# Input projections: bias tiles copied after the weight requests, two q/k weight tiles split ahead, first v weights split within the q/k block

## The chip, the cores and the metric

The kernel runs on one NeuronCore of a Trainium2 chip. The metric is the device time of one execution in microseconds (us); the three timed runs of the kernel before gave 1987.66, 1990.0 and 1991.83 us, median 1990.0 us. Engines are called PE (TensorE), PEld (its weight loads), ACT (ScalarE), DVE (VectorE), POOL (GpSimd) and SP (SyncE).

## What is computed

One decoder layer over 512 prompt tokens and 32 sample tokens, model width 1024. Only its first part matters here:

```python
u = rmsnorm(h, g_attn)
z = u @ w_in              # q, k, v of 8 forgetting heads | q, k, v of 8 dilated heads | 8 forget logits
logf = log_sigmoid(fz + b_f)          # 8 per token; summed along the tokens for the attention bias
o_fox = attention(qa, ka, va, cumulated logf)
o_dil = dilated attention(qb, kb, vb, rel_bias table)
h = h + [rms(o_fox) | rms(o_dil)] @ w_out
h = h + PEER(rmsnorm(h))              # 16384 single-neuron experts, top 16 per head
```

k, v and logf of all tokens are outputs as well. The bias table `rel_bias` gives, per dilated head, a 128 x 512 tile of biases and its turned twin; attention reads them from DRAM.

## The kernel before

The work is a row of blocks. Each block gives every engine its own instruction list, and the engines meet at the end of the block; inside it only semaphores order them. Every fp32 product is made of three matmuls (`mm3`, lines 225 to 227) of operands split in two: ACT copies the weights to a rounded high part (`hi`), DVE subtracts it from the weights for the low part (`lo`). So each weight tile goes DMA, ACT, DVE, PE.

The norm block (lines 298 to 386) turns the normalised tokens into `xhi`, `xlo`. It also loads the first two q/k weight tiles and writes the bias rows to DRAM (lines 334, 335).

The q/k block (lines 391 to 529) makes q and k transposed, in 8 turns m = 0..7. Each turn has two tiles of 128 columns, u = 0 (q) and u = 1 (k), of 512 KB each. PE's list is `product(0, 0)`, then a loop whose pass is `product(m, 1)`, `product(m+1, 0)`, `turn_k(m)`, and after the seven passes `product(7, 1)`, `turn_k(7)`. A product is 48 matmuls of 272 columns. `turn_k` transposes k back to token rows in 5 transposes, which DVE copies to `kn` (lines 472, 473) and POOL writes to the k outputs. POOL waits for each output to land before it frees `kn`, and for the last one before the block ends (line 529).

SP's list in this block begins with two transfers from DRAM to DRAM of 2 MB each, which spread the bias rows to the tiles `tile_dram` (line 414). Behind them come the loads of the 14 other q/k tiles, each waiting for the low split of the tile whose buffer it takes (lines 417, 418), and the loads of the first two v weight tiles of 1 MB each (line 420).

ACT's turn (lines 434 to 445) is: split hi of (m, 1), evacuate product (m, 0) to `qkT`, split hi of (m+1, 0), evacuate product (m, 1) to `kz`. DVE's turn (lines 464 to 473) is: split lo of (m, 1), split lo of (m+1, 0), wait for `kz` and copy it to `qkT`, wait for `turn_k(m)` and copy `kn`.

The v block (lines 531 to 612) makes v in 4 chunks of 256 columns. For each chunk PE does 5 token tiles of 24 matmuls into five accumulators `pv_acc` (line 277), and DVE copies each to `v` (line 533). `token_rows_product` (line 229) holds the lists of that product. PE waits for the low split of the chunk (`lo_done`, line 272) and for its accumulator to be free (`out_done`, line 275); the semaphore `out_done` is first raised to 5 by DVE in `first_on_vector` (line 257). DVE's list in the block is: `first_on_vector` (that raise, two low splits of v), the chain of the forget gate that turns the logits into `logf` and `cum` (lines 581 to 596, with ACT at lines 558 to 565), `on_vector` (the evacuations, and the low splits of chunks 2 and 3). ACT's list is two high splits of v (line 249), its gate steps, and the other high splits. SP's transfers of line 547, 548 and 241 wait for the end of the gate chain.

After it comes a barrier of all engines (line 616) and the attention block, where SP waits for the two bias transfers (line 724) and reads tiles from the fifth head pair on.

Of the kernel before, what the change touches and what calls it, by code (L numbers as in the profile page):

```python
# [32 lines left out]
P = 128  # L33
# [6 lines left out]
TT = SEQ // P + 1  # L40
# [28 lines left out]
def build(nc, A, O):  # L69
# [21 lines left out]
    with ctx:  # L91
# [134 lines left out]
            nc.tensor.matmul(out, a_hi, b_lo, start=False, stop=False)  # L226
            return nc.tensor.matmul(out, a_lo, b_hi, start=False, stop=last)  # L227

        def token_rows_product(st, tag, xhi, xlo, w, wld, w_dram, w_tiles, evacuate):


            CW = 256
            whi = sb(st, tag + "_whi", [P, 2, KD, CW], F32R)
            wlo = sb(st, tag + "_wlo", [P, 2, KD, CW], F32R)
            acc = [ps(st, f"{tag}_acc{t}", [P, CW]) for t in range(TT)]
            hi_done, lo_done, mm_done, out_done = (brief(f"{tag}_{n}") for n in ("hi_done", "lo_done", "mm_done", "out_done"))

            def on_sync(sp):
                for chunk in range(2, w_tiles):
                    sp.wait_ge(lo_done, chunk - 1)  # L240
                    sp.dma_start(w[:, chunk % 2], w_dram[chunk]).then_inc(wld[chunk % 2], 16)


            def on_scalar(act, chunks=range(w_tiles)):
                for chunk in chunks:
                    act.wait_ge(wld[chunk % 2], 16 * (chunk // 2 + 1))
                    if chunk >= 2:
                        act.wait_ge(mm_done, (chunk - 1) * TT)
                    nc.scalar.activation(whi[:, chunk % 2], w[:, chunk % 2], ACT.Copy).then_inc(hi_done, 1)

            def split_lo(dve, chunk):
                dve.wait_ge(hi_done, chunk + 1)
                nc.vector.tensor_tensor(wlo[:, chunk % 2], w[:, chunk % 2], whi[:, chunk % 2].bitcast(F32),
                                        ALU.subtract).then_inc(lo_done, 1)

            def first_on_vector(dve):
                dve.sem_inc(out_done, TT)
                split_lo(dve, 0)
                split_lo(dve, 1)

            def on_vector(dve):
                for chunk in range(w_tiles):
                    for t in range(TT):
                        if t == 2 and 1 <= chunk < w_tiles - 1:
                            split_lo(dve, chunk + 1)
                        dve.wait_ge(mm_done, chunk * TT + t + 1)
                        evacuate(t, chunk, acc[t]).then_inc(out_done, 1)

            def on_tensor(pe):
                with pe.Fori(0, w_tiles // 2) as j:  # L270
                    for u in range(2):
                        pe.wait_ge(lo_done, 2 * j + u + 1)
                        for t in range(TT):

                            pe.wait_ge(out_done, (2 * j + u) * TT + t + 1)
                            for k in range(KD):
                                last = mm3(acc[t][:], xhi[:, k, t * P:(t + 1) * P], xlo[:, k, t * P:(t + 1) * P],
                                           whi[:, u, k], wlo[:, u, k], k == 0, k == KD - 1)
                            last.then_inc(mm_done, 1)

            return on_sync, on_scalar, first_on_vector, on_vector, on_tensor


# [104 lines left out]
        w_early = sb(proj, "pv_w", [P, 2, KD, 256])  # L388
        w_loaded = [brief(f"pv_wld{u}") for u in range(2)]
        zf = ps(proj, "zf", [NH, 2, SEQ])  # L390
        with ExitStack() as st:
            w = w_qk
            whi = sb(st, "pwhi", [P, 2, KD, P], F32R)
# [14 lines left out]
            @block.sync  # L408
            def _(sp):

                sp.wait_ge(rows_done, 32)
                for turned, rows_of in enumerate((bass.AP(bias_dram.tensor, NH * DIST + P - 1, [[DIST, NH], [-1, P], [1, SEQ]]),
                                                  bass.AP(turned_dram.tensor, P - 1, [[DIST, NH], [-1, P], [1, SEQ]]))):
                    sp.dma_start(tile_dram[turned], rows_of).then_inc(tiles_done, 16)
                with sp.Fori(0, NH - 1) as m:
                    for u in range(2):
                        sp.wait_ge(lo_done, 2 * m + u + 3)
                        sp.dma_start(w[:, u], A["w_qk"][2 * m + 2 + u]).then_inc(wld[u], 16)
                for u in range(2):
                    sp.dma_start(w_early[:, u], A["w_v"][u]).then_inc(w_loaded[u], 16)  # L420


            @block.scalar
            def _(act):
                act.sem_inc(ev_done, 2)
                act.wait_ge(f_ld, 32)
                nc.scalar.activation(wfhi[:], wf[:], ACT.Copy).then_inc(f_hi, 1)

                def split(m, u):
                    act.wait_ge(wld[u], 16 * m + 16)  # L430
                    act.wait_ge(mm_done, 2 * m + u + 1)
                    nc.scalar.activation(whi[:, u], w[:, u], ACT.Copy).then_inc(hi_done, 1)

                def turn(m, last):
                    split(m, 1)
                    act.wait_ge(mm_done, 2 * m + 3)
                    nc.scalar.activation(qkT[:, 2 * m, :].rearrange("p (a b) -> p a b", a=2),
                                         zp[0][:, :, :HALF], ACT.Copy).then_inc(ev_done, 1)
                    if not last:
                        split(m + 1, 0)  # L440
                    act.wait_ge(mm_done, 2 * m + 4)
                    act.wait_ge(kt_done, m + 1)
                    act.wait_ge(kcopied, m + 1)
                    nc.scalar.activation(kz[:].rearrange("p (a b) -> p a b", a=2),
                                         zp[1][:, :, :HALF], ACT.Copy).then_inc(ev_done, 1)

                split(0, 0)
                with act.Fori(0, NH - 1) as m:
                    turn(m, False)
                turn(NH - 1, True)  # L450

            @block.vector
            def _(dve):
# [8 lines left out]
                    nc.vector.tensor_tensor(wlo[:, u], w[:, u], whi[:, u].bitcast(F32), ALU.subtract).then_inc(lo_done, 1)  # L462

                def turn(m, last):
                    split(m, 1)
                    if not last:
                        split(m + 1, 0)
                    dve.wait_ge(ev_done, 2 * m + 4)
                    nc.vector.tensor_copy(qkT[:, 2 * m + 1, :], kz[:]).then_inc(kcopied, 1)
                    dve.wait_ge(kt_done, m + 2)  # L470
                    dve.wait_ge(kn_free, m + 1)
                    nc.vector.tensor_copy(kn[:, 0:TT - 1], kp[:, 0:TT - 1])
                    nc.vector.tensor_copy(kn[:NS, TT - 1], kp[:NS, TT - 1]).then_inc(kn_done, 1)

                split(0, 0)
                with dve.Fori(0, NH - 1) as m:
                    turn(m, False)
                turn(NH - 1, True)
# [50 lines left out]
                pool.wait_ge(k_out, 32 * NH)  # L529

        with ExitStack() as st:
            def keep_v(t, chunk, acc):
                return nc.vector.tensor_copy(v[:, t, bass.ds(chunk * 256, 256)], acc[:])

            on_sync, on_scalar, first_on_vector, on_vector, on_tensor = token_rows_product(st, "pv", xhi, xlo, w_early, w_loaded, A["w_v"], 4, keep_v)
            gz, ga, ge, gu, gl, gd, gw = (sb(st, "g" + n, [NH, NT]) for n in ("z", "a", "e", "u", "l", "d", "w"))
            logf = sb(st, "logf", [NH, NT])
            cum = sb(st, "cum", [NH, SEQ])
# [5 lines left out]
            @block.sync  # L544
            def _(sp):
                sp.wait_ge(f_dve, 10)
                sp.dma_start(logf_dram, logf[:]).then_inc(f_out, 16)
                sp.dma_start(cum_dram, cum[:]).then_inc(f_out, 16)
                on_sync(sp)
                sp.wait_ge(f_dve, 11)  # L550
                sp.dma_start(O["lfp"].rearrange("(t p) h -> p t h", p=P), lf[:, 0:TT - 1]).then_inc(f_out, 16)
                sp.dma_start(O["lfs"], lf[:NS, TT - 1]).then_inc(f_out, 16)
                sp.wait_ge(f_out, 64)

            @block.scalar
            def _(act):
                on_scalar(act, range(2))
                nc.scalar.activation(gz[:].rearrange("p (a b) -> p a b", a=2), zf[:, :, :HALF], ACT.Identity,
                                     bias=bf[:]).then_inc(f_act, 1)
                act.wait_ge(f_act, 1)  # L560
# [2 lines left out]
                nc.scalar.activation(ge[:], ga[:], ACT.Exp, scale=-1.0).then_inc(f_act, 1)  # L563
                act.wait_ge(f_dve, 1)
                nc.scalar.activation(gl[:], gu[:], ACT.Ln).then_inc(f_act, 1)
                on_scalar(act, range(2, 4))

            @block.vector
            def _(dve):
                first_on_vector(dve)  # L570
                count = [0]

                def step(ins):
# [20 lines left out]
                nc.vector.tensor_tensor_scan(cum[:], ga[:, :SEQ], logf[:, :SEQ], 0.0, ALU.mult, ALU.add).then_inc(f_tr, 1)  # L594
                dve.wait_ge(f_tr, 2)
                step(nc.vector.tensor_scalar(cum[:], cum[:], -SCALE8, None, ALU.mult))
                on_vector(dve)
                dve.wait_ge(f_mm, 1)
                nc.vector.tensor_scalar(cumT[:], lp[:, TT:], 1.0 / SCALE8, None, ALU.mult)
                nc.vector.tensor_copy(lf[:, 0:TT - 1], lp[:, 0:TT - 1])  # L600
# [1 line left out]

            @block.tensor
            def _(pe):
                on_tensor(pe)
                pe.wait_ge(f_dve, 10)
                for t in range(TT - 1):
                    nc.tensor.transpose(lp[:, TT + t], cum[:, t * P:(t + 1) * P], ident[:NH, :NH])
# [1536 lines left out]
```

## Time and profile before

| | |
|---|---|
| median of 3 runs | 1990.0 us (1987.66 to 1991.83) |
| the profiled execution | 1990.47 us, span 1988.8 us from first to last instruction |
| PE busy | 1738.9 us, 87% of the span, 9914 matmuls |
| PEld busy | 1519.9 us, 76% |
| DVE, ACT, POOL busy | 1442.5, 689.4, 594.2 us |
| mean granted PE clock | 0.941 of full |

Start times are microseconds from the start of the span. The norm block ends at about 33 us, the q/k block's last PE instruction at 177.73, the v block's at 247.53. A timeline row gives the start, the duration, the engine, line and operation, what it writes and reads, and in brackets how long its engine had been idle before it and who released it. An engine that waits little is not yet the one that sets the end: one has to ask for each idle stretch of PE what came last.

### The profile page before, as it was taken

How to read it: one execution, taken by the hardware profiler on the slowest of the kernel's cores; microseconds unless marked ns; L12 is line 12 of the kernel's file. 1: busy time of each engine (PE TensorE's matmuls, PEld its weight loads, DVE VectorE, ACT ScalarE, POOL GpSimd, SP SyncE). 2: the span in 40 equal slices, each digit the busy share in tenths (PEclk: the TensorE clock that was granted, in tenths of full speed). 3: DMA queues.
4: the chain of work that ended last, by engine and by line, in shares of the span. 5: the costliest groups of instructions: out<-in, count | busy, mean ns of one | idle time of the engine just before them, and what ended most of it. 6: DMA issues, size and time to landing. Idle time of an engine off the chain costs nothing. (4 is left out here: it accounts for less than half of the span.)

```text
span 1988.8 us, 30525 instructions
## 1 busy us (share of the span) xinstructions
PE 1738.9 (87%) x9914; PEld 1519.9 (76%) x9914; DVE 1442.5 (73%) x3310; ACT 689.4 (35%) x912; POOL 594.2 (30%) x520
## 2 busy tenths in 40 slices
PE   5786988788799999996989989989499999999995
PEld 4786943347688888886988888888488888888883
DVE  3123346624467666677999999999698999999985
ACT  3112022202333333322545445445233333333333
POOL 0000072000134443434333333333333333333330
PEclk9888989889799999998999999999799999999997
DMA  4321182053133333333998998998899999999993
GB/s 142 111 80 70 43 265 75 16 213 122 63 109 109 122 108 108 112 108 127 331 362 327 349 362 327 338 366 326 305 384 383 385 385 385 384 385 385 385 385 115
DMA packets 195174, 470.30 MB, mean 236 GB/s; under 512 B 17922, under 2 KB 100482, under 8 KB 192558
## 3 DMA queue, kind: packets, MB, share of 16 engines
q1 hardware_dynamic: 124014, 240.30, 34.1%
q0 software_dynamic: 50944, 178.96, 24.4%
q10 hardware_dynamic: 20160, 50.34, 6.4%
q8 instruction: 30, 0.49, 0.1%
q14 instruction: 26, 0.21, 0.0%
HBM read 411.97 MB, written 61.32 MB: 238 GB/s over the span
## 5 line engine op out<-in xcount | busy, mean ns | idle before, releaser
L225 PE MATMUL hp<-mid_hi,uhi 128*128 128x384 f32 x1024 | 365.3, 357 | 40.6 <-POOL ulo L1284 31.1
L226 PE MATMUL hp<-mid_lo,uhi 128*128 128x384 f32 x1024 | 354.5, 346 | 0.0
L227 PE MATMUL hp<-mid_hi,ulo 128*128 128x384 f32 x1024 | 352.4, 344 | 0.0
L225 PE MATMUL va<-vhi,ahi 128*128 128x512 f32 x768 | 300.0, 391 | 21.3 <-DVE alo L1923 21.3
L226 PE MATMUL va<-vlo,ahi 128*128 128x512 f32 x768 | 299.5, 390 | 0.0
L227 PE MATMUL va<-vhi,alo 128*128 128x512 f32 x768 | 299.5, 390 | 0.0
L1939 POOL DMA_INDIRECT gathered<-in_v_experts,idx_row x160 | 186.3, 1164 | 329.6 <-DVEq L1894 289.2
L1644 POOL DMA_INDIRECT gathered<-in_u_rows,idx_row x160 | 169.9, 1062 | 300.8 <-DVE hrow L1699 199.8
L225 PEld LDWEIGHTS hp<-mid_hi,uhi 128*128 128x128 f32 x1024 | 201.3, 197 | 46.7 <-POOL ulo L1284 33.3
L1280 ACT ACTIVATE uhi<-uw 128x1024 fp32r<-128x1024 f32 x128 | 135.5, 1059 | 236.3 <-PE hp L227 143.6
L226 PEld LDWEIGHTS hp<-mid_lo,uhi 128*128 128x128 f32 x1024 | 200.7, 196 | 0.0
L227 PEld LDWEIGHTS hp<-mid_hi,ulo 128*128 128x128 f32 x1024 | 200.4, 196 | 0.0
L1868 ACT ACTIVATE vhi<-vw 128x1024 fp32r<-128x1024 f32 x128 | 134.8, 1053 | 151.9 <-DMA vw<-in_v_experts 147.8
L225 PEld LDWEIGHTS va<-vhi,ahi 128*128 128x128 f32 x768 | 144.7, 188 | 52.1 <-issue 22.0
L1699 DVE CUSTOM_DVE_ANT_0 gathered<-gathered,x2p 128x1024 f32<-128x1024 f32 x150 | 177.6, 1214 | 9.2 <-DMA gathered<-in_u_rows,idx_row 5.5
L1284 POOL TENSOR_TENSOR ulo<-uw,uhi 128x1024 fp32r<-128x1024 f32 x54 | 131.4, 2440 | 171.1 <-ACT uhi L1280 171.1
L1918 DVE TENSOR_TENSOR vlo<-vw,vhi 128x1024 fp32r<-128x1024 f32 x128 | 156.2, 1220 | 17.1 <-ACT vhi L1868 16.9
L226 PEld LDWEIGHTS va<-vlo,ahi 128*128 128x128 f32 x768 | 144.7, 188 | 30.1
L227 PEld LDWEIGHTS va<-vhi,alo 128*128 128x128 f32 x768 | 144.6, 188 | 30.1
L1891 DVE SCALAR_TENSOR_TENSOR acc<-gathered,crow,acc 128x1024 f32<-128x1024 f32 x128 | 164.2, 1282 | 0.0
L1622 PE MATMUL ggp<-og,oh 128*128 128x128 f32 x768 | 107.8, 284 | 36.9 <-DVE og L1690 36.9
L1622 PEld LDWEIGHTS ggp<-og,oh 128*128 128x128 f32 x768 | 98.2, 194 | 50.3 <-DVE og L1690 50.3
(318 smaller groups left out, 3279.9 us busy)
## 6 DMA issues: line engine op xcount, KB each, us to landing
uw<-in_u_experts SPq DMA_DIRECT2D x128, 512.0 KB
vw<-in_v_experts SPq DMA_DIRECT2D x128, 512.0 KB
hidden_values<-gelu_out ACTq DMA_DIRECT2D x128, 192.0 KB
gate_matrix<-gst ACTq DMA_DIRECT2D x12, 2048.0 KB
hd<-hidden_values SPq DMA_DIRECT2D x32, 768.0 KB
gt<-gate_matrix SPq DMA_DIRECT2D x32, 768.0 KB
pw<-in_w_qk SPq DMA_DIRECT2D x16, 512.0 KB, 3.8
qw<-in_w_query SPq DMA_DIRECT2D x16, 512.0 KB, 4.3
```

The costliest lines, as they stand in the source:

```text
L225: nc.tensor.matmul(out, a_hi, b_hi, start=first, stop=False)
L226: nc.tensor.matmul(out, a_hi, b_lo, start=False, stop=False)
L227: return nc.tensor.matmul(out, a_lo, b_hi, start=False, stop=last)
L1280: nc.scalar.activation(uhi[:, i], uw[:, i], ACT.Copy).then_inc(u_hi, 1)
L1284: nc.gpsimd.tensor_tensor(ulo[:, i], uw[:, i], uhi[:, i].bitcast(F32), ALU.subtract).then_inc(u_lo, 1)
L1622: last = nc.tensor.matmul(gp[i % 2][:, k], oh[:, i % RING, k], og[:, i % RING, k], start=True, stop=True)
L1644: nc.gpsimd.indirect_dma_start(gb[:, b], None, u_table, bass.IndirectOffsetOnAxis(ap=idx_row[:, slot, b:b + 1], axis=0)).then_inc(gathered ...
L1699: nc.vector.tensor_tensor_reduce(out=gb[:, b], in0=gb[:, b], in1=x2p[:, b // SG], scale=1.0, scalar=0.0, op0=ALU.mult, op1=ALU.add, accum_ ...
L1868: nc.scalar.activation(vhi[:, c], vw[:, c], ACT.Copy).then_inc(s["vhi"], 1)
L1891: nc.vector.scalar_tensor_tensor(acc0[:], gb[:, c], crow[:, q, c:c + 1], acc0[:], ALU.mult, ALU.add).then_inc(s["s0"], 1)
L1918: nc.vector.tensor_tensor(vlo[:, c], vw[:, c], vhi[:, c].bitcast(F32), ALU.subtract).then_inc(s["vlo"], 1)
L1939: nc.gpsimd.indirect_dma_start(gb[:, b], None, v_table, bass.IndirectOffsetOnAxis(ap=idx_row[:, slot, b:b + 1], axis=0)).then_inc(gathered ...
```

## The change

Three moves, all in the input projections; no arithmetic is added or left out.

1. On SP the two transfers of the bias tiles go from the front of its q/k list to its end, behind the loads of the 14 q/k tiles and the two v tiles.
2. On DVE, tile (0, 1) is split ahead of the loop, and each turn splits (m+1, 0) before the copy of `kz` and (m+1, 1) right after it, instead of (m+1, 1) at the start of the next turn, behind the `kn` copies.
3. The high and low splits of v chunks 0 and 1 go from the front of the v block into the last turn of the q/k block: ACT's behind the evacuation of product (7, 0), DVE's in the place of the split it no longer has there. For that the `pv` split buffers are allocated earlier. The first raise of `out_done` goes from `first_on_vector` to the front of `on_vector`.

```diff
@@ token_rows_product
             def first_on_vector(dve):
-                dve.sem_inc(out_done, TT)
                 split_lo(dve, 0)
                 split_lo(dve, 1)
 
             def on_vector(dve):
+                dve.sem_inc(out_done, TT)
                 for chunk in range(w_tiles):
@@ q/k block, sync
-                sp.wait_ge(rows_done, 32)
-                for turned, rows_of in enumerate((bass.AP(bias_dram.tensor, NH * DIST + P - 1, [[DIST, NH], [-1, P], [1, SEQ]]),
-                                                  bass.AP(turned_dram.tensor, P - 1, [[DIST, NH], [-1, P], [1, SEQ]]))):
-                    sp.dma_start(tile_dram[turned], rows_of).then_inc(tiles_done, 16)
                 with sp.Fori(0, NH - 1) as m:
                     for u in range(2):
                         sp.wait_ge(lo_done, 2 * m + u + 3)
                         sp.dma_start(w[:, u], A["w_qk"][2 * m + 2 + u]).then_inc(wld[u], 16)
                 for u in range(2):
                     sp.dma_start(w_early[:, u], A["w_v"][u]).then_inc(w_loaded[u], 16)
-
+                sp.wait_ge(rows_done, 32)
+                for turned, rows_of in enumerate((bass.AP(bias_dram.tensor, NH * DIST + P - 1, [[DIST, NH], [-1, P], [1, SEQ]]),
+                                                  bass.AP(turned_dram.tensor, P - 1, [[DIST, NH], [-1, P], [1, SEQ]]))):
+                    sp.dma_start(tile_dram[turned], rows_of).then_inc(tiles_done, 16)
@@ q/k block, scalar, turn
-                    if not last:
+                    if last:
+                        v_split_hi(act, range(2))
+                    else:
                         split(m + 1, 0)
@@ q/k block, vector, turn
-                    split(m, 1)
-                    if not last:
+                    if last:
+                        v_split_first(dve)
+                    else:
                         split(m + 1, 0)
                     dve.wait_ge(ev_done, 2 * m + 4)
                     nc.vector.tensor_copy(qkT[:, 2 * m + 1, :], kz[:]).then_inc(kcopied, 1)
+                    if not last:
+                        split(m + 1, 1)
...
                 split(0, 0)
+                split(0, 1)
@@ v block, scalar
-                on_scalar(act, range(2))
                 nc.scalar.activation(gz[:].rearrange("p (a b) -> p a b", a=2), zf[:, :, :HALF], ACT.Identity,
                                      bias=bf[:]).then_inc(f_act, 1)
@@ v block, vector
-                first_on_vector(dve)
...
                 step(nc.vector.tensor_scalar(cum[:], cum[:], -SCALE8, None, ALU.mult))
-                on_vector(dve)
+                v_evacuate(dve)
```

`v_split_hi`, `v_split_first`, `v_evacuate` are the new names of `on_scalar`, `first_on_vector`, `on_vector`.

## Rows read from the trace of the kernel before

**Rows 1.** Busy time by engine in the q/k and v stretches (windows view).

```profile
core 0: us, PE busy (x) PEld busy (x) DVE busy (x) ACT busy (x) POOL busy (x), PEclk, DMA share, GB/s
33.06:177.73 144.67, 120.67 (x856) 115.55 (x856) 27.93 (x38) 24.87 (x32) 9.39 (x14) 0.91 0.30 108
177.73:247.53 69.80, 58.84 (x489) 58.62 (x489) 28.51 (x38) 12.68 (x10) 1.31 (x2) 0.90 0.09 35
```

**Rows 2.** What PE waited for, 33 to 250: total us, times, longest.

```profile
PE zp L225 <- DVE pwlo L462: 23.3, 8, 8.1
PE pv_acc L225 <- DVE pv_wlo L253: 11.0, 1, 11.0
```

**Rows 3.** Timeline of PE, its restarts and its transposes.

```profile
60.62 0.59 PE L225 MATMUL zp<-xhi,pwhi 128*128 128x272 f32 x1 [8.10 <-DVE pwlo L462]
69.46 0.71 PE L501 MATMUL kp<-ident,kz 128*128 128x128 f32 x5
72.35 0.39 PE L225 MATMUL zp<-xhi,pwhi 128*128 128x272 f32 x1 [2.18 <-DVE pwlo L462]
168.44 0.39 PE L225 MATMUL zp<-xhi,pwhi 128*128 128x272 f32 x1 [2.10 <-DVE pwlo L462]
...
188.69 0.58 PE L225 MATMUL pv_acc<-pv_whi,xhi 128*128 128x256 f32 x1 [10.96 <-DVE pv_wlo L253]
```

**Rows 4.** PE alone, windows from restart to end of products: busy, clock, DMA.

```profile
60.62:69.46 8.84, 8.84 (x48) 0.66 0.18 61
72.35:86.00 13.65, 13.65 (x96) 0.87 0.30 97
88.89:101.01 12.12, 12.12 (x97) 1.00 0.31 110
168.44:176.25 7.81, 7.80 (x48) 0.78 0.13 36
188.69:192.69 4.00, 4.00 (x18) 0.50 0.02 4
```

**Rows 5.** Timeline of ACT.

```profile
58.17 1.06 ACT L432 ACTIVATE pwhi<-pw 128x1024 fp32r<-128x1024 f32 x1 [10.90 <-DMA pw<-in_w_qk]
80.71 1.06 ACT L432 ACTIVATE pwhi<-pw 128x1024 fp32r<-128x1024 f32 x1
184.31 3.71 ACT L249 ACTIVATE pv_whi<-pv_w 128x2048 fp32r<-128x2048 f32 x2 [7.40 <-PEq L391]
187.93 0.69 ACT L558 ACTIVATE gz<-zf,bf 8x544 f32<-8x544 f32 x1
```

**Rows 6.** Timeline of DVE.

```profile
80.97 0.44 DVE L469 COPY qkT<-kz 128x544 f32 x1 [7.62 <-ACT kz L444]
86.75 0.69 DVE L472 COPY kn<-kp 128x512 f32<-128x512 f32 x1 [5.33 <-PE kp L501]
87.55 2.34 DVE L462 TENSOR_TENSOR pwlo<-pw,pwhi 128x1024 fp32r<-128x1024 f32 x2
186.25 4.49 DVE L253 TENSOR_TENSOR pv_wlo<-pv_w,pv_whi 128x2048 fp32r<-128x2048 f32 x2 [7.61 <-ACT pv_whi L249]
201.94 0.42 DVE L596 TENSOR_SCALAR cum<-cum 8x512 f32<-8x512 f32 x1
218.95 0.42 DVE L533 COPY v<-pv_acc 128x256 f32<-128x256 f32 x1 [2.38 <-PE pv_acc L227]
221.75 0.42 DVE L533 COPY v<-pv_acc 128x256 f32<-128x256 f32 x1 [2.38 <-PE pv_acc L227]
```

**Rows 7.** SP's queue: the bias transfers and what stands behind them.

```profile
33.24 0.78 SPq L414 DMA_DIRECT2D bias_tiles<-bias_rows  x1
38.30 115.58 SPq L418 DMA_DIRECT2D pw<-in_w_qk  x14
```

**Rows 8.** All engines, 36 to 48, with only the bias transfers moving.

```profile
36.00:48.00 12.00, 12.00 (x98) 10.78 (x97) 0.10 (x1) 0.63 (x1) 0.00 (x0) 1.00 0.53 197
```

**Rows 9.** Transfers issued 151 to 166, median us from issue to landing.

```profile
pv_w<-in_w_v SPq DMA_DIRECT2D x2, 1024.0 KB, 7.2
pw<-in_w_qk SPq DMA_DIRECT2D x1, 512.0 KB, 3.8
out_kwp<-kn POOLq DMA_DIRECT2D x1, 256.0 KB, 3.5
```

More of the change, by code:

```diff
@@ L227, in mm3, with token_rows_product @@
             return nc.tensor.matmul(out, a_lo, b_hi, start=False, stop=last)
-        def token_rows_product(st, tag, xhi, xlo, w, wld, w_dram, w_tiles, evacuate):
+        def token_rows_product(st, tag, xhi, xlo, w, wld, w_dram, w_tiles, evacuate, acc):
             CW = 256
@@ L234, in token_rows_product @@
             wlo = sb(st, tag + "_wlo", [P, 2, KD, CW], F32R)
-            acc = [ps(st, f"{tag}_acc{t}", [P, CW]) for t in range(TT)]
             hi_done, lo_done, mm_done, out_done = (brief(f"{tag}_{n}") for n in ("hi_done", "lo_done", "mm_done", "out_done"))
@@ L390, in build, with keep_v @@
         zf = ps(proj, "zf", [NH, 2, SEQ])
+        v_acc = []
+        def keep_v(t, chunk, acc):
+            return nc.vector.tensor_copy(v[:, t, bass.ds(chunk * 256, 256)], acc[:])
+        v_loads, v_split_hi, v_split_first, v_evacuate, v_products = token_rows_product(
+            proj, "pv", xhi, xlo, w_early, w_loaded, A["w_v"], 4, keep_v, v_acc)
         with ExitStack() as st:
@@ L531, in build @@
         with ExitStack() as st:
-            def keep_v(t, chunk, acc):
-                return nc.vector.tensor_copy(v[:, t, bass.ds(chunk * 256, 256)], acc[:])
-            on_sync, on_scalar, first_on_vector, on_vector, on_tensor = token_rows_product(st, "pv", xhi, xlo, w_early, w_loaded, A["w_v"], 4, keep_v)
+            v_acc += [ps(st, f"pv_acc{t}", [P, 256]) for t in range(TT)]
             gz, ga, ge, gu, gl, gd, gw = (sb(st, "g" + n, [NH, NT]) for n in ("z", "a", "e", "u", "l", "d", "w"))
@@ L548, in _ @@
                 sp.dma_start(cum_dram, cum[:]).then_inc(f_out, 16)
-                on_sync(sp)
+                v_loads(sp)
                 sp.wait_ge(f_dve, 11)
@@ L565, in _ @@
                 nc.scalar.activation(gl[:], gu[:], ACT.Ln).then_inc(f_act, 1)
-                on_scalar(act, range(2, 4))
+                v_split_hi(act, range(2, 4))
             @block.vector
             def _(dve):
-                first_on_vector(dve)
                 count = [0]
@@ L604, in _ @@
             def _(pe):
-                on_tensor(pe)
+                v_products(pe)
                 pe.wait_ge(f_dve, 10)
```

## The prediction

> **What bounds the kernel now.** I read the windows view first. It cuts the span where PE's work changes: the q/k stretch takes 144.67 us with PE busy for 120.67, the v stretch 69.80 us with 58.84 busy [rows 1]. No other engine is busy for half of either, and the DMA engines move little, so PE sets both stretches and the question is what it waits for and at which clock it runs. The table of waits answers the first: 23.3 us of idle PE in 8 waits for DVE's low split of a q/k tile, the longest 8.1, and one wait of 11.0 for the low split of v [rows 2]. The timeline places them: 8.10 us before 60.62, once; 2.18 us in each of the six loop passes whose product follows a `turn_k`, and 2.10 before the last product, at 168.44 [rows 3]. The clock answers the second. The reader should lay the passes of two products beside each other: 12.12 us where the granted clock is 1.00, 13.65 us where it is 0.87 [rows 4]; of the six, four (from 72.35, 103.90, 120.44 and 136.98) last 13.65 and two 12.12. Clock 1.00 is 2.4 GHz, and the 0.50 of the first 4 us of the v products is 1.2 GHz [rows 4]; every stretch at the low level follows an idle stretch of PE. So a stall is paid twice here, in idle time and in slow matmuls behind it.
>
> **The opening stall (SP's move).** The third q/k tile reached SP's queue at 38.30, behind two transfers of 2 MB that were issued from 33.24 on [rows 7]. ACT waited 10.90 us for it and could split it only at 58.17 [rows 5]. After the change SP waits only for the low split of tile (0, 0) and asks for the third tile near 35; a tile takes about 3.8 us to land [rows 9], so it is there before product (0, 0) frees its buffers. The stall of 8.10 goes, and product (1, 0) takes half of 12.12, 6.06 us, instead of the 8.84 from 60.62 to 69.46 at mean clock 0.66 [rows 3, 4]. Worth 8.10 + 2.78 = 10.88 us. What is late next there: nothing; both splits of that tile take 2.3 us and a product of 6 us runs meanwhile.
>
> **The stall in each turn (DVE's move).** DVE does `kn`, then two splits in 2.34 us, and only the second is the one that PE waits for [rows 6]. It could have been done long before: ACT's high split of (m+1, 1) runs at 80.71, right after `kz` [rows 5], while DVE copies at 80.97 and then sits idle for 5.33 us until `turn_k` [rows 6]. After the change the split runs from about 81.8 to 83.0 in that picture, 3 us before the product then running ends, with `turn_k`'s 0.71 more as slack; the split of (m+2, 0) comes behind the `kn` copies, about 3 us after the product that frees it, under a product of 6.06. So I cost both splits at nothing. All seven stalls go, 6 x 2.18 + 2.10 = 15.2. With PE never idle I take the clock to stay at 1.00 as it does from 88.89, so four passes give 1.53 each, 6.1, and the last product 7.81 - 6.06 = 1.75 [rows 4]. Together 23.0 us.
>
> Two costs that the stall may have covered have no row of their own. One is the loop's way back. In the v block PE also loops, and DVE's evacuations at the last tile of chunk 1 and the first of chunk 2, on the two sides of that way back, start 2.80 us apart [rows 6], as within a chunk; its bounds are 0 and the 2.18 it could hide in, and I take 0, the nearest row. The Trainium skill (Advanced Engine Details and Errata, section Control Flow Timing) puts a compare-and-branch at about 108 ns; an estimate from it is 0.8 us over seven passes, which the sum leaves out, since the row shows nothing of it. The other is the load of the next tile: from the split that frees its buffer to the product that frees the split buffers it has about 10 us, against 3.8.
>
> PE's end in the q/k block thus goes from 177.73 to 177.73 - 10.9 - 23.0 = 143.8.
>
> **The end of the q/k block.** The v splits now stand in the last turn. On ACT, 3.71 us behind the evacuation of product (7, 0) [rows 5] end near 4.4 us into the 6.8 before product (7, 1) is done. On DVE, `kn` of turn 6 ends 1.7 us after product (7, 0), the two splits of v take 4.49 [rows 6] from about 2.8, and end near 7.2, when `kz` is just written at about 7.5. They cost nothing, with 0.3 us to spare on DVE. If that cover were gone they would delay the last `kn` by their excess. The v weights are requested with the last q/k tile, near 120, and need 7.2 us [rows 9]; they are wanted at 136.
>
> Behind them SP now issues the bias transfers, at about 121. They alone keep 0.53 of the DMA engines busy at 197 GB/s [rows 8], so 4.19 MB take 21 us; after the weights have landed near 128.5 this gives an end near 150. The transposes of turns 6 and 7 end near 136 and 144, and their outputs leave some 2 us later, within that time, and the block cannot end before the last has landed. Before, the block switched at 184.31, 6.58 us after PE's last instruction [rows 1, 5]. What the mixture costs, no row shows. The nearest has an output of 256 KB landing in 3.5 us with weight loads issued around it [rows 9], nearly no cost; the other end is an output that waits until the copies are through, which for the last one is 3 us and for that of turn 6, which holds up the next `kn` copy, up to 6. I take 1, near the row, and keep 0 to 6. The first row that speaks for more is that half of the engines is busy all the time [rows 8]. The Trainium skill (DMA: Bandwidth & Descriptors, section Queues, rings and completion order) says that an engine alternates between its queues packet by packet, so an output would be interleaved and not stand behind the whole copy; by that rule the sum would stay in the lower half of my bounds. SP itself waits for nothing after its last issue, and attention asks for the tiles only much later.
>
> The v block therefore begins at 143.8 + 6.6 + 1 = 151.4 instead of 184.31.
>
> **The v block: a wait that takes the place of the one removed.** Before, PE waited for ACT and DVE to split chunk 0: 188.69 - 184.31 = 4.38 us after the block began [rows 3, 5]. That is gone. But PE also needs `out_done`, and its first raise now stands behind the gate chain in DVE's list. Everything in the block waits for it: PE's four chunks, all evacuations, and with them the end. The chain's length is in the trace: ACT's first gate step starts at 187.93 and DVE's last ends at 201.94 + 0.42 = 202.36 [rows 5, 6], 14.43 us, a pure chain of ACT and DVE steps with no DMA and no PE in it. Before, it ran beside PE's chunk 0. Now ACT starts it with the block, and PE starts at 14.5 us instead of 4.4: 10.1 us lost. From there PE has its 58.84 us of work as before [rows 1], which already hold the slow start (4.00 us at 0.50 after 10.96 idle [rows 3, 4]); PE's idle stretch is about 22 us now, and the restart after 8.10 idle lost 2.78 us, that is 5.6 at the low level, some 2 more than here, so this term is good to 1 us. Loads and splits of chunk 2 start with the chain's end as before and have all of chunk 0 to hide in.
>
> **The sum.** 33.9 gained in the q/k block, 10.1 lost in the v block, 1 for the shared DMA engines: 22.8 us. The attention block begins behind a barrier of all engines and PE's end at 247.53 comes near 224.7, so all later work, none of which was requested earlier, moves by the same amount. The profiled execution took 1990.47 us for a span of 1988.8; it should come to about 1967.7, and the median of 1990.0 to 1967.2, forecast 1967.
>
> **The rivals.**
> (a) The stalls shrink but stay. If a way back, a semaphore or the split still holds PE for about half of the 2.18 in each turn, 7.7 us stay, and so does the slow clock behind them, 7.9: gain 7.2, 1983. For it: small idle stretches did lower the clock in four of six passes. Against: the slack of 3 us above. 10%.
> (b) The seven turns gain nothing, because each wait is taken over by another (a tile load, `kn` behind POOL's outputs). Then only the opening's 10.9 stands against 10.1 + 1: 1990. Against: a tile lands in 3.8 us and an output in 3.5 [rows 9], in a turn of 12.8. 3%.
> (c) The k outputs are held up by the bias copies to the far end, 4 to 6 us: 1970 to 1972. 8%.
> (d) PE is not held by the gate chain, since the accumulators are free in fact and something else raises the count. Then 14 us more are gained: 1953. The lists say otherwise. 3%.
> (e) Slower: after the long idle stretch at the front of the v block the clock does not come back. At the 1.2 GHz level 18 matmuls took 4.00 us [rows 4], so a chunk's 120 take 26.7, against 14.0 at full clock (five evacuations 2.80 apart [rows 6]). Four chunks cost 51 us more, of which 2 are in the sum already: 1967 + 49 = 2016. It decides from two chunks at the low level on, 25 us. Against it: after 8.10 and after 10.96 us of idle the clock was back within 6 us. 4%.
> The forecast itself has 72%.
>
> **The numbers.** Low end: no DMA cost (1966), 2 for a shorter slow start, 2 for the spread of runs: 1962. High end: 6 of DMA cost (1972), and 5 for the loop, the branch and spread: 1977. The range holds the forecast and (c) and a part of (a). About 0.2%, 4 us, is what a measurement of this kernel can tell from no change. Faster by more than that: 0.72 + 0.10 + 0.08 + 0.03 = 0.93; within: 0.03 (b); slower: 0.04 (e).
>
> **What would show it.** In the profile after: PE's waits for `pwlo` gone from the q/k stretch (now 23.3); every pass of two products 12.1 us at clock 1.00; the last transposes near 144; a switch of blocks near 151; then a PE wait of about 21 to 22 us ended by DVE's `cum` or by no named instruction, with the first v product right behind the gate chain; PE's end of v near 225. If passes last 13 us or more, the clock step failed; if the block switches at 155 or later, the DMA step; if v starts within 5 us of the switch, the reading of `out_done` was wrong.

## The result and the profile after

The changed kernel took 1971.31 us (median of 4 runs, 1968.57 to 1978.38) against 1988.83 for the kernel before on the same occasion: ratio 0.9913, interval 0.989 to 0.9936, 17.5 us less. The forecast was 1967, range 1962 to 1977. The profiled execution took 1978.38 us, the slowest of the four, with a span of 1976.8. Six further runs of the same kernel (e1, below) had a median of 1969.73. Line numbers differ from the kernel before: 414 is 425, 472 is 481, 501 is 511, 558 is 564, 596 is 601, and the evacuation of v at 533 is 392; behind line 600 they are 5 higher.

The windows view of the q/k and v stretches of the kernel after, the rows that answer to [rows 1]:

```profile
core 0: us, PE busy (x) PEld busy (x) DVE busy (x) ACT busy (x) POOL busy (x), PEclk, DMA share, GB/s
32.28:141.36 109.08, 108.37 (x856) 105.21 (x856) 33.70 (x40) 28.48 (x34) 9.37 (x14) 1.00 0.38 131
141.36:225.93 84.57, 59.45 (x490) 59.22 (x489) 24.31 (x36) 9.07 (x8) 1.31 (x2) 0.84 0.12 45
```

The q/k stretch went from 144.67 us to 109.08 and PE is busy in all but 0.7 of it, at a mean granted clock of 1.00. The v stretch grew from 69.80 to 84.57 with the same work in it. PE's timeline shows where:

```profile
166.48 0.58 PE L225 MATMUL pv_acc<-pv_whi,xhi 128*128 128x256 f32 x1 [25.12 <-DVEq L259]
232.42 0.80 PE L766 MATMUL S<-qkT 64*128 64x128 f32 x4 [6.49 <-ACT identr L889]
```

Between `turn_k(7)` and the first v product PE waits 25.12 us, before 10.96 [rows 3], and the one that releases it is DVE's queue at line 259, which is the raise of `out_done`. The timelines of SP, DVE, POOL and ACT show what the 25.12 us are made of:

```profile
118.33 0.81 SPq L421 DMA_DIRECT2D pv_w<-in_w_v  x2
119.19 0.79 SPq L425 DMA_DIRECT2D bias_tiles<-bias_rows  x1
120.02 9.12 SPq L425 DMA_DIRECT2D bias_tiles<-turned_bias_rows  x1
...
141.95 0.69 DVE L481 COPY kn<-kp 128x512 f32<-128x512 f32 x1 [0.92 <-POOLq L538]
144.29 0.52 POOL L536 DMA_DIRECT2D out_kws<-kn  x1
151.94 0.70 ACT L564 ACTIVATE gz<-zf,bf 8x544 f32<-8x544 f32 x1 [11.39 <-PEq L396]
165.96 0.41 DVE L601 TENSOR_SCALAR cum<-cum 8x512 f32<-8x512 f32 x1
```

The block switches at 151.94, 10.58 us behind PE's last q/k instruction (6.58 before), and the gate chain runs from there to 166.37, 14.43 us as before [rows 5, 6]; PE starts 0.1 us later.

A loop pass of the q/k block, and the first 4 us of the v products (PE alone, against [rows 4]):

```profile
58.06:70.63 12.57, 12.57 (x103) 1.00 0.33 106
120.90:133.40 12.50, 12.50 (x103) 1.00 0.73 284
166.48:170.48 4.00, 4.00 (x18) 0.50 0.57 199
```

These passes hold the transposes too: from one evacuation of q to the next 12.57 us, where before it was 15.0 or 16.5. The transposes take 0.46 us of it, the time from their start to that of the next product:

```profile
57.77 0.71 PE L511 MATMUL kp<-ident,kz 128*128 128x128 f32 x5
58.23 0.37 PE L225 MATMUL zp<-xhi,pwhi 128*128 128x272 f32 x1
```

PE's end in the v block came from 247.53 to 225.93, 21.6 us sooner. Only 12.0 of them are left in the span of this execution. Where they went is the second question of the experiments. Most was lost at once, in the first 24 us of attention; the kernel before and then the kernel after, PE alone from its first attention matmul on:

```profile
253.98:277.98 24.00, 23.47 (x117) 0.85 0.94 317
```

```profile
232.42:256.42 24.00, 23.92 (x76) 0.55 0.94 315
```

A mean clock of 0.85 means 7.2 us at 1.2 GHz, one of 0.55 means 21.6. PE got through 117 matmuls before and through 76 after in the same time. The first reciprocal of attention (line 849, then 854) starts 25.5 us behind the block's constants before, 31.3 us after: 5.8 us gone. The other 3.8 us went in small amounts behind it: 1.5 in the rest of attention, 2.3 in the blocks after it.

### The profile page after: what moved, and what is told of

The parts are those of the page before. It is cut to its first block and busy times, and to the rows that moved or that the text cites. A ratio compares the mean times of both kernels' runs of the same rounds, so it can differ in the third digit from the quotient of the medians.

```text
span 1976.8 us, 30524 instructions
## 1 busy us (share of the span) xinstructions
PE 1736.0 (88%) x9914; PEld 1514.8 (77%) x9914; DVE 1444.3 (73%) x3310; ACT 688.9 (35%) x912; POOL 594.3 (30%) x520
## 5 line engine op out<-in xcount | busy, mean ns | idle before, releaser
L225 PEld LDWEIGHTS hp<-mid_hi,uhi 128*128 128x128 f32 x1024 | 201.1, 196 | 47.1 <-POOL ulo L1289 33.9
## 6 DMA issues: line engine op xcount, KB each, us to landing
hd<-hidden_values SPq DMA_DIRECT2D x32, 768.0 KB, 12.7
gt<-gate_matrix SPq DMA_DIRECT2D x32, 768.0 KB, 16.4
```

The source lines that it names most:

```text
L225: nc.tensor.matmul(out, a_hi, b_hi, start=first, stop=False)
```

## The experiments

All runs are compared with the kernel before run beside them; the 95% interval of a ratio reaches 0.15 to 0.27% to either side, which is 3 to 5 us.

**e1: the changed kernel again.** No edit.

> The changed kernel once more, nothing altered. In its first profile PE's end in the v block came 21.6 us sooner than before, but the span was only 12.0 us shorter: 5.8 us were lost in the first 30 us of attention, where the granted clock stood at 0.50 for 22 us instead of 7.6. Theory A (the clock's return after an idle stretch varies from run to run): this profile loses another amount there, between 0 and 6 us, the span moves with it, and the median is near 1969. Theory B (the change causes that loss): the low clock at the start of attention lasts about 22 us again and the span is near 1977.

Measured: 1969.73 us (6 runs, 1966.04 to 1973.94), ratio 0.9898 (0.9878 to 0.9917), span of the profile 1972.4. PE's end of v at 225.44. PE alone over the first 24 us of attention:

```profile
231.92:255.92 24.00, 24.00 (x84) 0.61 0.94 313
```

About 18.5 us at the low level (by quarters of a microsecond) and not 21.6, the first reciprocal 4.2 us late and not 5.8. Neither theory is settled by it: the length changes for one and the same kernel, but it is long again. PE's wait before v was 24.45 us here.

**e8: the kernel before again**, for the same question.

> The kernel before once more, for a second profile of the start of attention. Theory A (how long the clock stays at 0.50 after the switch to attention changes from run to run, whatever the kernel): a length other than the 7.2 us of its first profile, between 6 and 22. Theory B (the long stretches of 13 to 22 us belong to the kernels whose v splits were moved): about 7 us again.

Measured: 1990.32 us (8 runs, 1985.1 to 1992.41), ratio 1.000 (0.9986 to 1.0015).

```profile
253.91:277.91 24.00, 23.71 (x95) 0.72 0.95 312
```

About 13.5 us at the low level where the first profile of the same kernel had 7.2, and 95 matmuls instead of 117. The first reciprocal of attention came 2.2 us later for it, the end of the span 1.5. So the length changes from execution to execution for the kernel before too; theory B's "about 7 again" is wrong. Over all profiles of this study the mean clock of those 24 us was 0.85, 0.72, 0.86 (e3) and 0.85 (e4) where the v splits stay in the v block and PE waits 11 to 13 us at its front, and 0.55, 0.61, 0.73 (e2), 0.84 (e5), 0.86 (e6), 0.60 (e7), 0.72 (e9) and 0.72 (e10) for the kernels with the moved splits. Both groups spread. That the moved splits make the long stretches more frequent is neither shown nor excluded by so few.

**e2: `out_done` raised ahead of the gate chain**, in the changed kernel:

```diff
@@ token_rows_product
+            def raise_free(dve):
+                dve.sem_inc(out_done, TT)
+
             def on_vector(dve):
-                dve.sem_inc(out_done, TT)
@@ v block, vector
+                v_raise(dve)          # ahead of the gate chain
                 count = [0]
```

> The changed kernel with the first raise of out_done at the very front of DVE's list in the v block, ahead of the gate chain, and nothing else altered. Theory: PE's 25 us wait before the v products is the last kn output and the switch (10.6 us) plus the gate chain (14.5 us); with the raise ahead of it PE starts within 0.5 us of the switch, the chain hides beside chunk 0 (16 us), and PE's end of v comes 14.2 us sooner: median near 1957. Rival: the v products cannot start sooner for another reason (instruction lists, PSUM still read by the gate, the split weights): no gain, 1971. Second rival: DVE frees no accumulator until the chain ends, so chunk 1 is held up: more than 1 us of PE idle behind chunk 0, gain under 12.

Measured: 1954.24 us (5 runs, 1952.96 to 1958.44), ratio 0.9832 (0.9812 to 0.9852). Waits of PE and the first evacuation on DVE:

```profile
PE pv_acc L225 <- DVEq L259: 10.4, 1, 10.4
```

```profile
152.27 0.70 ACT L566 ACTIVATE gz<-zf,bf 8x544 f32<-8x544 f32 x1 [11.22 <-PEq L398]
166.75 0.42 DVE L394 COPY v<-pv_acc 128x256 f32<-128x256 f32 x1
```

PE's wait fell from 25.12 to 10.43 us: v starts with the switch, 0.04 us behind ACT's first gate step. The gate chain still takes its 14.4 us, but it ends at 166.72 while PE is in chunk 0, and PE has no second wait, so the accumulators come free in time. PE's end of v is at 211.02, 14.9 us sooner than in the changed kernel; the median is 15.5 us under that of e1, which ran beside it. The order of two entries in DVE's list is worth almost as much as the whole change gained.

**e3: SP's move alone**, on the kernel before.

```diff
-                sp.wait_ge(rows_done, 32)
-                for turned, rows_of in enumerate((...)):
-                    sp.dma_start(tile_dram[turned], rows_of).then_inc(tiles_done, 16)
                 with sp.Fori(0, NH - 1) as m:
...
+                sp.wait_ge(rows_done, 32)
+                for turned, rows_of in enumerate((...)):
+                    sp.dma_start(tile_dram[turned], rows_of).then_inc(tiles_done, 16)
```

> The kernel before with SP's move alone (bias transfers behind the weight loads). Theory: the stall of 8.1 us before product (1, 0) and its slow clock go (10.9 us), the six stalls of 2.18 stay, and the last k outputs are not held up, since the turns are longer and the bias transfers end before them, or by at most 4 us: 1978 to 1982. Rival: the loop's first pass inherits the stall (the third tile is still late): no gain, 1989.

Measured: 1981.93 us (11 runs, 1979.26 to 1985.8), ratio 0.996 (0.9946 to 0.9975), 7.7 us less. Waits of PE:

```profile
PE zp L225 <- DVE pwlo L462: 15.2, 7, 2.2
PE pv_acc L225 <- DVE pv_wlo L253: 12.8, 1, 12.8
```

The wait of 8.1 is gone, the seven of 2.2 stay, and the wait before v is 12.8 instead of 11.0. PE's last q/k instruction ends at 166.58, 11.15 us sooner; the forecast's term was 10.9. PE's end of v is only 9.75 us sooner, at 237.78, since the bias copies now touch the end of the block: its last small output landed 4.0 us after its issue, against 2.2 before, and the block switches 8.45 us behind PE's last q/k instruction instead of 6.58.

**e4: DVE's order alone**, on the kernel before.

```diff
                 def turn(m, last):
-                    split(m, 1)
                     if not last:
                         split(m + 1, 0)
                     dve.wait_ge(ev_done, 2 * m + 4)
                     nc.vector.tensor_copy(qkT[:, 2 * m + 1, :], kz[:]).then_inc(kcopied, 1)
+                    if not last:
+                        split(m + 1, 1)
...
                 split(0, 0)
+                split(0, 1)
```

> The kernel before with DVE's order alone (tile (m+1, 1) split behind the kz copy). Theory: all seven stalls of 2.1 to 2.2 us and the low clock behind them go, while the opening stall stays: passes of 12.6 us at clock 1.00, 23 us less, 1966. Rival (small stalls cost only themselves, the clock drops anyway): 15 us less, 1974.

Measured: 1965.41 us (5 runs, 1961.82 to 1968.39), ratio 0.9876 (0.9856 to 0.9897), 24.3 us less, more than the whole change. Waits of PE, and PE alone from 78.00, well behind the opening stall, to the end of the products (the clock is back at 1.00 by 68):

```profile
PE pv_acc L225 <- DVE pv_wlo L253: 11.0, 1, 11.0
PE zp L225 <- DVE pwlo L462: 8.1, 1, 8.1
```

```profile
78.00:152.45 74.45, 74.45 (x599) 1.00 0.34 114
```

The seven small waits are gone and 74 us run without a gap at full clock. This answers the rival, by which small stalls cost only themselves: the seven waits sum to 15.2 us, but the gain to PE's end of v is 22.95 (224.58 against 247.53), or 23.9 from the start of the q/k work, which came 0.9 us later in this execution. The q/k stretch itself shrank by 24.7: 15.2 of waits, 7.9 of the clock that no longer falls [rows 4] and 1.6 of shorter transposes; 0.8 of it was lost again in the v block.

**e5: the v part alone**, on the kernel before. The changed kernel, with these two lists as they were before:

```diff
@@ q/k block, sync: the bias transfers in front again
@@ q/k block, vector, turn
+                    split(m, 1)
                     if last:
                         v_split_first(dve)
...
-                    if not last:
-                        split(m + 1, 1)
...
                 split(0, 0)
-                split(0, 1)
```

> The kernel before with the third part of the change alone (v splits in the last q/k turn, out_done raised behind the gate chain); SP's and DVE's order as before. Theory: the q/k block ends as before, the v products start 14.5 us behind the switch instead of 4.4, so 10.1 us slower: 2000. Rival (the chain would have held up PE before as well, by the evacuations): within 2 us of 1990.

Measured: 1997.68 us (6 runs, 1995.11 to 2001.95), ratio 1.0047 (1.0029 to 1.0065), 8.9 us slower.

```profile
PE pv_acc L225 <- DVEq L259: 21.5, 1, 21.5
```

Taken alone this part is a loss: PE's wait before v is 21.46 us instead of 10.96. The 10.5 us are the forecast's 10.1 and 0.3 more: the switch is 6.9 us behind PE's last q/k instruction and not 6.58, although no copy runs there.

**e6: the bias transfers in the v block**, from the changed kernel, to separate the 4 us at the switch.

```diff
@@ q/k block, sync: the wait on rows_done and the two transfers removed
@@ v block, sync
+                sp.wait_ge(rows_done, 32)
+                for turned, rows_of in enumerate((...)):
+                    sp.dma_start(tile_dram[turned], rows_of).then_inc(tiles_done, 16)
                 sp.wait_ge(f_dve, 10)
                 sp.dma_start(logf_dram, logf[:]).then_inc(f_out, 16)
```

> The changed kernel with the two bias transfers at the front of SP's list in the v block. Theory: the 10.6 us between PE's last q/k instruction and the switch hold 4 us of k outputs that share the DMA engines with the bias copies; with the copies behind the switch it is 6.6 again, as before the change, and nothing in the v block needs the DMA engines soon: 4 us less than the changed kernel, 1966. Rival: the 4 us are the time that SP or the v splits take, not the sharing: switch still 10 us behind PE, 1970. If the loads of v chunk 2 are held up by the copies, PE waits behind chunk 1.

Measured: 1967.8 us (6 runs, 1965.58 to 1971.99), ratio 0.9894 (0.9877 to 0.9912); the change itself had 1971.3 and 1969.7, so in the medians the difference is no more than hinted at. The profile shows the earlier switch. ACT's first step behind the switch, and PE's wait:

```profile
148.87 0.70 ACT L564 ACTIVATE gz<-zf,bf 8x544 f32<-8x544 f32 x1 [7.74 <-PEq L396]
```

```profile
PE pv_acc L225 <- DVEq L259: 21.5, 1, 21.5
```

The switch is 6.91 us behind PE's last q/k instruction (141.96), not 10.58. The transfers themselves say why; issued in the last turn, median us from issue to landing, kernel after and then e6:

```profile
out_kwp<-kn POOLq DMA_DIRECT2D x1, 256.0 KB, 2.9
out_kws<-kn POOLq DMA_DIRECT2D x1, 16.0 KB, 5.3
```

```profile
out_kwp<-kn POOLq DMA_DIRECT2D x1, 256.0 KB, 2.8
out_kws<-kn POOLq DMA_DIRECT2D x1, 16.0 KB, 2.2
```

The large output is hardly disturbed by the copies; the small one, 16 KB behind it, lands 3.1 us later, and it is the last thing the block waits for. The kernel before, whose last outputs meet no copy, and turn 6 of the kernel after (issued at 136.25, 12 us before the copies end near 148.6) show the same two figures:

```profile
out_kws<-kn POOLq DMA_DIRECT2D x1, 16.0 KB, 2.2
```

```profile
out_kws<-kn POOLq DMA_DIRECT2D x1, 16.0 KB, 5.6
```

Turn 6's landing also holds up DVE's last `kn` copy: it starts 0.59 us behind PE's last transpose, before 0.04. That 0.55 and the 3.1 are the 3.7 us by which the switch moves between the kernel after and e6.

**e7: e2 and e6 together.**

> Both repairs of the changed kernel together: out_done raised ahead of the gate chain, bias transfers at the front of SP's list in the v block. Theory: 14.2 + 4 us less than the changed kernel, 1951; PE idle 6.9 us between the blocks. Rival: now chunk 2's load, behind the copies in the same queue and asked for at the chain's end, comes late: PE idle of some us before chunk 2 and a gain of 14 us or less.

Measured: 1955.91 us (5 runs, 1953.22 to 1961.15), ratio 0.9829 (0.9811 to 0.9847). Waits of PE, and ACT's high split of chunk 2:

```profile
PE pv_acc L225 <- DVEq L259: 7.0, 1, 7.0
PE pv_acc L225 <- DVE pv_wlo L251: 1.1, 1, 1.1
```

```profile
176.84 1.92 ACT L247 ACTIVATE pv_whi<-pv_w 128x2048 fp32r<-128x2048 f32 x1 [21.46 <-DMA pv_w<-in_w_v]
```

The rival named beforehand is there, small: the wait at the switch fell by 3.5 us, and a new one of 1.1 us came before chunk 2, whose weights were requested behind the copies. From PE's last q/k instruction to its end of v it is 67.2 us, in e2 69.1; the median did not follow.

**e9: the v loads in front of everything**, in e7's v block, and **e10: e2 again** beside it.

```diff
@@ v block, sync, against e7
+                v_loads(sp)
                 sp.wait_ge(rows_done, 32)
...
                 sp.dma_start(cum_dram, cum[:]).then_inc(f_out, 16)
-                v_loads(sp)
```

> e7 with the loads of v chunks 2 and 3 at the very front of SP's list in the v block, ahead of the bias transfers and of the logf and cum transfers. Theory: e7's wait of PE before chunk 2 (1.09 us, its weights landed behind the bias copies) goes, the switch stays 6.9 us behind PE's last q/k instruction, and PE's end of v comes 66 us after that instruction (e2: 69.1, e7: 67.2): median 3 us under e2's, 1951. Rival: logf and cum, now behind 6 MB in the same queue, hold up the end of the v block: the end of v comes as late as in e7 or the attention block starts over 6.5 us behind it.

> e2 once more, beside e9 on the same chip. Theory: 1954, and e9 3 us under it. Rival: the difference between them is below what the start of attention and the later stages vary by from run to run, and the medians cannot be told apart.

Measured: e9 1952.66 us (5 runs, 1947.16 to 1955.67), ratio 0.9804 (0.9777 to 0.9831); e10 1955.9 us (5 runs, 1952.71 to 1960.05), ratio 0.9832 (0.9807 to 0.9857). In e9 the wait before chunk 2 is gone and PE needs 65.2 us from its last q/k instruction (141.85) to its end of v (207.03), 3.9 less than e2's 69.1 and 3.7 less than e10's 68.9. The end of the block is not held up: attention starts 6.48 us behind it as always. The medians differ by 3.2 us as expected, with intervals that overlap. e9 has the lowest median, but it and e2 are each 35.4 us under the kernel before that ran beside them, so only the profiles put e9 ahead.

## Why the prediction was right, point by point

- **The opening stall**, forecast 10.9 us: the third tile is there in time, no wait of PE behind 32.28 in the q/k loop, and e3 alone has PE's last q/k instruction 11.15 sooner. Right.
- **The seven stalls with the clock behind them**, forecast 23.0: e4 alone moves PE's end of v by 22.95. In the changed kernel the passes are shorter than I took them, 12.57 us against 12.12 + 0.71 = 12.83, since the transposes cost 0.46 and not 0.71 when the next product follows at once; 6 x 0.26 = 1.6 us. PE's q/k stretch shrank by 35.6 and not 33.9. Right, slightly low; no stall is left, so rivals (a) and (b) are out, and the loop's way back costs nothing that shows.
- **The v splits under the last turn**, forecast at nothing with 0.3 us to spare on DVE: DVE was through with both splits 0.26 us before `kz` was written. Right.
- **The shared DMA engines**, forecast 1 us with bounds 0 to 6: it is 4.0, the term of the sum that was mis-sized. The step that failed is "the nearest has an output of 256 KB landing in 3.5 us": I read the large output's row and not the small one's. The last to land is the 16 KB output, 5.3 us from issue instead of 2.2, and DVE's last `kn` copy started 0.55 us late behind the output before it. e6 takes the copies away and has 3.7 us of the 4.0 back; the other 0.3 us are there in e5, e7 and e9 too (the switch 6.9 us behind PE), so they come with the moved v splits and not with the copies, and no run shows why. The price and the time are those of rival (c), 4 to 6 us and 1970 to 1972, to which I gave 8%; its picture fits by half, for the mixture does not queue an output behind the whole copy: in turn 6, with 12 us of copying still to come, the small output landed in 5.6 us. The Trainium skill (DMA: Bandwidth & Descriptors, section Queues, rings and completion order) has an engine alternate between its queues packet by packet, and so far the trace agrees; the inference I hung on it, that the sum stays in the lower half of the bounds, was wrong. The sign I had named for this step, a switch at 155 or later, did not come, because PE's q/k work ended 2.4 us sooner than forecast; what shows the miss is PE's wait of 25.12 us, forecast 21 to 22.
- **The wait that takes the place of the one removed**, forecast 10.1 us lost: PE's releaser is the raise of `out_done` behind the chain; e5 alone shows 10.5 us more wait and 8.9 us more time, e2 takes it out and gains 14.9 to the end of v. Right; rival (d) is out.
- **The slow start of v**: PE's v work took 59.45 us instead of 58.84, within the 1 us allowed. The clock was back 5.7 us behind the restart, so rival (e) is out.
- **The sum** was 22.8 us to PE's end of v and the trace has 21.6 (of which 0.8 lie in the norm block, which the change doesn't touch): 35.6 - 10.2 - 4.0 - 0.6 = 20.8. That this is within 2 us of the forecast is in part luck: the q/k block gave 1.7 more than forecast, the shared DMA engines took 3.0 more.
- **"All later work moves by the same amount"** did not hold in the profiled executions: the spans are 12.0 us (kernel after) and 16.4 us (e1) shorter where PE's end of v is 21.6 and 22.1 sooner. Of that, 5.8 and 4.2 us went in the slow start of attention. That start is at the low clock for 7 to 22 us, and in the kernel before for 7.2 in one execution and 13.5 in another; so a part of the shortfall is what executions of one kernel differ by, and the first profile of the kernel before was short there by luck. The medians do not refute the step: they are 17.5 and 19.9 us less, with intervals of 12.7 to 21.9 and 16.5 to 24.3 that both hold the 20.8. Whether a mean loss of a microsecond or two belongs to the change stays open: no run moved the start of attention alone.

## What to carry to other kernels

When work is moved ahead of a chain of small steps, look at every semaphore raise that stays behind the chain: one line in the wrong place here turned a gain of 4 us into a loss of 10, and moving it back was worth 15. A stall of 2 us in each turn of a PE-bound loop deserves more attention than its sum says, since the clock fell behind it in four of six turns; splitting the next operand in the idle stretch of the helper engine cost nothing. A transfer moved off the start of a block can land on its end, and here the smallest output that the block waits for, not the largest, showed the cost.

## What was not expected of the hardware

- After the switch to attention the granted clock stayed at 0.50 for 6.7 to 21.6 us (e3, kernel after), and for 7.2 and 13.5 in two executions of one kernel. Behind the restart with the v products it was 2.9 to 6.2 us (e2, e1); the idle stretch before it does not settle the length, for after the same 21.5 us it was 3.9 in e5 and 6.1 in e6.
- A 16 KB output issued right behind one of 256 KB took 2.2 us with nothing else moving and 4.0 to 5.6 beside a copy from DRAM to DRAM, while the 256 KB one took 2.8 without the copy and 2.9 to 3.0 with it. Where the v weights moved as well (kernel after, 122.9), the two took 6.0 and 4.4.
- The bias copies left the other half of the DMA engines' time free and were not slowed by an output: 0.53 busy at 197 GB/s alone [rows 8], and 52.5% for SP's queue while the last outputs ran beside it (kernel after, 142 to 146).
- The granted clock does not tell all: in the first 3 us of the q/k stretch the matmuls start 0.23 us apart, later 0.125, while the granted clock is given as 1.00 throughout (kernel after, 32.28 to 35.4, behind 4.07 us of idle PE). This holds in the kernel before too, and no run shows why.
